# The per-head means of an encoder's projection: full-precision matmul, or two passes over split squares

## What is computed

```
xn = rms_norm(x, norm_mix)
proj = xn @ w_in                      # columns: q | k | v | ssm | two gates
q = rms_norm(q per head of 64, q_norm)    # mean over 64 channels of q*q
k = rms_norm(k per head of 64, k_norm)
q, k = rope(q), rope(k)
```

## Time and profile before

| what | value |
|---|---|
| three timed executions | 2587.70, 2590.16, 2594.99 us |
| median | 2590.16 us |
| the profiled execution, its own time | 2588.01 us |
| its span, first to last instruction | 2586.2 us |
| TensorE busy, matmuls | 2543.9 us, 98% |
| VectorE busy | 1615.3 us, 62% |
| ScalarE busy | 1044.8 us, 40% |
| POOL busy | 1306.3 us, 51% |
| mean of TensorE's granted clock | 0.995 of full speed |

### The profile page before, as it was taken

How to read it: one execution, slowest core, us unless ns; L and a number is a source line. 1 busy time by engine, 2 the same in 40 slices (tenths; PEclk the granted TensorE clock), 3 DMA queues, 4 the chain that set the end, 5 groups by cost and what they waited for, 6 DMA issues and landing times.

```text
span 2586.2 us, 38172 instructions
## 1 busy us (share of the span) xinstructions
PE 2543.9 (98%) x11174; PEld 2094.0 (81%) x11174; DVE 1615.3 (62%) x1790; ACT 1044.8 (40%) x1513; POOL 1306.3 (51%) x899
## 2 busy tenths in 40 slices
PE   7999999999899999999999999999999999999999
PEld 5777788888778888868888888788888878888887
DVE  7996288888688888866673353566453436673351
ACT  5444021221577777764442232344332334432231
POOL 3334756463567666654444444444444444454444
PEclk9999999999999999999999999999999999999999
DMA  4334132222552121124222334432222454222323
GB/s 167 110 122 143 68 90 88 86 85 76 138 146 75 46 65 49 43 92 153 98 97 95 100 119 162 158 116 97 98 98 95 137 183 146 97 94 95 99 96 122
DMA packets 132188, 274.27 MB, mean 106 GB/s; under 512 B 32896, under 2 KB 45696, under 8 KB 131968
## 3 DMA queue, kind: packets, MB, share of 16 engines
q1 hardware_dynamic: 132096, 273.12, 33.0%
HBM read 222.10 MB, written 48.76 MB: 105 GB/s over the span
## 4 chain that ended last, share of the span: by engine, by line
PE 55%; DMA 1%; POOL 0%; issue 0%; ACT 0%; DVE 0%; SPq 0%; DVEq 0%; POOLq 0%; ACTq 0%
PE t_ps L62 18%; PE t_ps L64 18%; PE t_ps L63 18%; DMA t_wraw<-w_tail_t 1%; POOL t_wlo L1942 0%; ACT t_whi L1961 0%; DVE t_x L2123 0%; PE t_ps L2157 0%; SPq L1917 0%; SPq L1882 0%; DVEq L2122 0%; SPq L1861 0%; POOLq L1941 0%; SPq L57 0%; DVEq L2046 0%
## 5 line engine op out<-in xcount | busy, mean ns | idle before, releaser
L1942 POOL TENSOR_TENSOR t_wlo<-t_wraw,t_whi 128x1024 fp32r<-128x1024 f32 x265 | 669.1, 2525 | 787.4 <-ACT t_whi L1961 787.4
L62 PE MATMUL t_ps<-block,t_whi 128*128 128x512 f32 x1920 | 748.4, 390 | 0.6 <-POOL t_wlo L1942 0.6
L64 PE MATMUL t_ps<-block,t_wlo 128*128 128x512 f32 x1920 | 746.9, 389 | 0.0
L63 PE MATMUL t_ps<-block,t_whi 128*128 128x512 f32 x1920 | 746.9, 389 | 0.0
L1961 ACT ACTIVATE t_whi<-t_wraw 128x1024 fp32r<-128x1024 f32 x265 | 280.2, 1057 | 551.4 <-PE t_ps L64 489.1
L62 PEld LDWEIGHTS t_ps<-block,t_whi 128*128 128x128 f32 x1920 | 360.4, 188 | 76.7 <-issue 2.2
L63 PEld LDWEIGHTS t_ps<-block,t_whi 128*128 128x128 f32 x1920 | 360.4, 188 | 75.8 <-issue 0.7
L64 PEld LDWEIGHTS t_ps<-block,t_wlo 128*128 128x128 f32 x1920 | 360.4, 188 | 74.7
L1552 POOL TENSOR_TENSOR a_plo<-a_p,a_phi 128x512 fp32r<-128x512 f32 x240 | 309.1, 1300 | 148.0 <-DVE a_phi L1671 140.7
L2123 DVE TENSOR_TENSOR t_x<-t_ps,t_x 128x512 f32 (+1 forms) x96 | 66.4, 692 | 373.8 <-PE t_ps L64 373.8
L2117 DVE TENSOR_TENSOR block<-t_tc,block 128x512 f32 x96 | 232.8, 2425 | 30.1 <-ACT block L2022 29.6
(11 more groups left out here) (244 smaller groups left out, 4055.4 us busy)
## 6 DMA issues: line engine op xcount, KB each, us to landing
t_wraw<-w_tail_t SPq DMA_DIRECT2D x266, 512.0 KB, 3.3
block<-roped_scratch SPq DMA_DIRECT2D x144, 128.0 KB, 2.7
w_raw<-w_in_t SPq DMA_DIRECT2D x32, 512.0 KB, 3.8
proj_scratch<-s_gate SPq DMA_DIRECT2D x48, 256.0 KB, 2.1
t_graw<-proj_scratch SPq DMA_DIRECT2D x24, 512.0 KB, 3.8
roped_scratch<-p_r_hi SPq DMA_DIRECT2D x30, 256.0 KB, 2.0
roped_scratch<-p_r_lo SPq DMA_DIRECT2D x30, 256.0 KB, 2.3
mix_scratch<-a_o SPq DMA_DIRECT2D x48, 128.0 KB, 2.4
```

The source lines that it names most:

```text
L62: pe.matmul(out, whi, xhi, start=start, stop=False)
L63: pe.matmul(out, whi, xlo, start=False, stop=False)
L64: return pe.matmul(out, wlo, xhi, start=False, stop=stop)
L1942: pool.tensor_tensor(w_lo[s][:], w_raw[s][:], f32(w_hi[s][:]), ALU.subtract).then_inc(wlo_ready, 1)
```

## The change

The squares are no longer given to a full-precision matmul. ScalarE squares a tile into `sw` and copies it, rounded to float32r, into `sq_hi`; POOL subtracts the two into `sq_lo`; TensorE makes the mean of two float32r matmuls that accumulate, one for each half. The mean matrix is loaded into `hmean_in` and copied into a float32r `hmean`. `sw` now holds first the square of one tile and later the swapped channels of another, so VectorE waits for the low half before it swaps, and ScalarE waits for a sum before it squares. POOL's order in a step is the low half and then the sine product of three steps before; its loop is cut into a first pair, four looped pairs and a rest of three sine products. To make room the buffer `o` of attention goes into the memory that is free after the gates, with a wait for the stores of the gates, and two squares of the input's norm go into other buffers.

```diff
-        self.o = [ctx.enter_context(nc.sbuf_tensor(f"a_o{s}", [HEAD, BLK], F32)) for s in range(2)]
+        self.o = [sb(f"a_o{s}", [HEAD, BLK]) for s in range(2)]
...
-        sq = sb("p1_sq", [P, 2, BLK])
-        hmean = sb("p1_hmean", [P, P])
+        hmean_in, hmean = sb("p1_hmean_in", [P, P]), sb("p1_hmean", [P, P], F32R)
+        sq_hi, sq_lo = (sb(f"p1_{n}", [P, 2, BLK], F32R) for n in ("sq_hi", "sq_lo"))
-        squares = [sq[:, 0], sq[:, 1], f32(r_lo[:, 0]), f32(r_lo[:, 1])]
+        squares = [rs[:, 2 * BLK:], qn[:, 1], f32(r_lo[:, 0]), f32(r_lo[:, 1])]
...
 ScalarE, pair():
+                    if first:
+                        act.wait_ge(rope_in, 48)
+                        act.activation(hmean[:], hmean_in[:], ACT.Copy).then_inc(hmean_set, 1)
...
-                            act.activation(sq[:, r % 2], stage[r // 3][:, cols(r % 3)],
+                            if not first or r >= 4:
+                                act.wait_ge(sum_ready, 6 * i + (r - 3))
+                            act.activation(sw[:, r % 2], stage[r // 3][:, cols(r % 3)],
                                            ACT.Square).then_inc(hsq_ready, 1)
+                            act.wait_ge(hsq_ready, 6 * i + (r + 1))
+                            act.activation(sq_hi[:, r % 2], sw[:, r % 2], ACT.Copy).then_inc(hsq_hi_ready, 1)
...
 POOL:
+                def square_low(i, r):
+                    pool.wait_ge(hsq_hi_ready, 6 * i + (r + 1))
+                    pool.tensor_tensor(sq_lo[:, r % 2], sw[:, r % 2], f32(sq_hi[:, r % 2]),
+                                       ALU.subtract).then_inc(hsq_lo_ready, 1)
+                for r in range(6):
+                    square_low(0, r)
+                    if r >= ROPE_LAG:
+                        sine(0, r - ROPE_LAG)
+                with pool.Fori(1, QK_PAIRS) as i:
                     for r in range(6):
-                        pool.wait_ge(sw_ready, 6 * i + (r + 1))
-                        pool.tensor_tensor(sw[:, r % 2], sw[:, r % 2], table[:, 1, cols(r % 3)],
-                                           ALU.mult).then_inc(sin_ready, 1)
+                        square_low(i, r)
+                        sine(i, r - ROPE_LAG)
+                for r in range(6 - ROPE_LAG, 6):
+                    sine(QK_PAIRS - 1, r)
...
 VectorE, rope():
                     dve.wait_ge(qn_ready, n + (k + 1))
+                    last = isinstance(i, int) and i == QK_PAIRS
+                    dve.wait_ge(hsq_lo_ready, NQK if last else n + (k + 3))
                     alone(dve, dve_turn)
                     dve.stream_shuffle(sw[:, s], qn[:, s], SWAP).then_inc(sw_ready, 1)
...
 TensorE, head_mean():
-                    pe.wait_ge(hsq_ready, 6 * i + (k + 1))
+                    pe.wait_ge(hsq_lo_ready, 6 * i + (k + 1))
...
-                    pe.matmul(mean[:, k % 2], hmean[:], sq[:, k % 2], start=True,
+                    pe.matmul(mean[:, k % 2], hmean[:], sq_hi[:, k % 2], start=True, stop=False)
+                    pe.matmul(mean[:, k % 2], hmean[:], sq_lo[:, k % 2], start=False,
                               stop=True).then_inc(hmean_ready, 1)
...
 attention, VectorE:
+                for c in range(NBLK):
+                    dve.wait_ge(st.gates[c], 16 * (2 * KD) + 16)
                 dve.memset(f32(v2[1][:, :, :, HEAD:P]), 0.0).then_inc(ones_set, 1)
```

More of the change, by code:

```diff
@@ L351, in project @@
         hsq_ready = sem("p1_hsq_ready")
+        hmean_set = sem("p1_hmean_set")
+        hsq_hi_ready = sem("p1_hsq_hi_ready")
+        hsq_lo_ready = sem("p1_hsq_lo_ready")
         hmean_ready = sem("p1_hmean_ready")
@@ L448, in _ @@
                     sp.dma_start(dst[:], src).then_inc(par_in, 16)
-                sp.dma_start(hmean[:], head_mean_d).then_inc(rope_in, 16)
+                sp.dma_start(hmean_in[:], head_mean_d).then_inc(rope_in, 16)
                 sp.dma_start(head_gain[:], qk_gain).then_inc(rope_in, 16)
@@ L603, in _, with sine @@
                 pool.wait_ge(rope_in, 48)
-                with pool.Fori(0, QK_PAIRS) as i:
+                def square_low(i, r):
+                    pool.wait_ge(hsq_hi_ready, 6 * i + (r + 1))
+                    pool.tensor_tensor(sq_lo[:, r % 2], sw[:, r % 2], f32(sq_hi[:, r % 2]),
+                                       ALU.subtract).then_inc(hsq_lo_ready, 1)
+                def sine(i, r):
+                    pool.wait_ge(sw_ready, 6 * i + (r + 1))
+                    pool.tensor_tensor(sw[:, r % 2], sw[:, r % 2], table[:, 1, cols(r % 3)],
+                                       ALU.mult).then_inc(sin_ready, 1)
+                for r in range(6):
[3 more added lines that the diff above has]
+                with pool.Fori(1, QK_PAIRS) as i:
                     for r in range(6):
-                        pool.wait_ge(sw_ready, 6 * i + (r + 1))
-                        pool.tensor_tensor(sw[:, r % 2], sw[:, r % 2], table[:, 1, cols(r % 3)],
-                                           ALU.mult).then_inc(sin_ready, 1)
+                        square_low(i, r)
+                        sine(i, r - ROPE_LAG)
+                for r in range(6 - ROPE_LAG, 6):
+                    sine(QK_PAIRS - 1, r)
                 n_link = [0]
@@ L862, in pair @@
                                 if first:
-                                    pe.wait_ge(rope_in, 48)
+                                    pe.wait_ge(hmean_set, 1)
                                 head_mean(i, k)
@@ L1376, in attention @@
         den = [sb(f"a_den{s}", [HEAD, BLK]) for s in range(2)]
-        o = st.o
+        o = fore.o
         ST_BANK, O_BANK, MX_BANK = 0, 2, 4
```

## The result

The changed kernel takes 2610.6 us (median of 4, 2609.5 to 2613.1) against 2589.8 us of the kernel before (median of 4). The ratio is 1.0078, with a 95% interval of 1.0066 to 1.0091: **slower by 20.8 us**. The profiled execution took 2611.1 us, its span is 2609.3 us. TensorE's matmuls are busy 2544.0 us, 97% of the span (98% before): the engine now stands idle for parts of the projection.

What follows compares the result with a forecast made beforehand. TensorE sets the pace, VectorE right behind; the change makes VectorE the bound of these pairs. Steps 20.4 us and first pair 3.1 us later, POOL's set-up ends the block 18 us late: 2608 us, range 2592 to 2622.

Steps and rivals of the forecast that it cites:

- The step times: VectorE's query and key steps: plain (no weight split) from 5.20 to 6.24 us, split from 6.37 to 7.92 us.
- the 23 steps: Second pair's first eviction to fifth pair's sixth: 16 plain and 7 split steps, 155.3 us, 20.4 more than before.
- the predicted 3.1: First pair's three roped steps: about 0.5, 1.04 and 1.55 us more, 3.1 us together.
- TensorE's gain: Two-pass means save TensorE 0.42 us a step, 12.5 us offered over 30 means; arrival depends on VectorE.
- What costs nothing: New waits of ScalarE and VectorE, the mean-matrix copy and attention's extra wait: no cost, save a few hundredths for a check.
- ScalarE's copies: 30 copies to the high half, about 0.63 us each: no cost of their own, but they stand ahead of the low half.
- The end of the block: Projection's end: POOL's state set-up, not VectorE's last weight split, ends the block, at 334.5 us.
- the 18: The projection block ends 18 us later, at 334.5 instead of 316.6 us, and nothing behind takes it back.
- The rival that the gain arrives: Low halves cost VectorE under 0.29 us a step, TensorE stays the bound, 12.5 us come off: 2578 us; chance 0.10.
- the argument against it: Against that rival: the square can't precede its eviction; the high half comes at 2.0 us, when the window is nearly over.
- the offsets: Times of a step's instructions from its eviction, taken from the kernel's own steps; gave 1.04 us more plain, 1.55 split.
- whether the shuffle blocks POOL: If VectorE's one-input shuffle blocked POOL, the low half would start 0.2 us later in plain steps, some 3 us in all.

Runs made afterwards that it cites:

- e1: Changed kernel without POOL's low half, both passes of a mean taking the high half: 2582.0 us, against 2591.4 of the kernel before.
- e2: Changed kernel with low halves still made, but the mean one full-precision matmul of the high half alone: 2612.5 us.
- e4: Changed kernel with the square in a buffer of its own, so the shuffle no longer waits for the low half: 2611.8 us.
- e11: Kernel before with only attention's buffer `o` moved and the wait for the gates' stores added, one execution: 2591.9 us.
- e5: e4 with VectorE scaling before it evicts and POOL's low half moved behind the sine product, beside the eviction: 2597.1 us.
- e3: Changed kernel with POOL subtracting one column and filling the rest of the low half by two memsets: 2586.8 us.
- e12: Kernel before with only the 12 small angle instructions of VectorE moved from behind pair 0 to before pair 4: 2587.7 us.
- e9: e5 with pair 0 in its old order, pair 1's first low half not held back, and the angle instructions before pair 4: 2587.4 us.

## Why the prediction was right

Forecast 2608.0 in 2592 to 2622, slower with 0.75; measured 2610.6. By its steps:

- **The step times.** Plain 6.24 predicted, 6.15 measured; split 7.92 and 7.84. The mechanism was the one named, the cosine product held in plain steps and L763 ahead of the low half in split ones. Both were 0.08 to 0.09 too long, 16 x 0.09 + 7 x 0.08 = 2.0 us; three plain steps took 6.30, which gives 0.5 back, so the 23 steps took 153.8 instead of 155.3. Pair 0 cost 4.25 us, 1.3 of it a later first eviction (54.15), and 2.95 of the predicted 3.1.
- **TensorE's gain.** 0.42 us a step offered (e1: 0.39), nothing arrived: e2 gives it back and loses nothing.
- **What costs nothing.** The waits (e4), the copy of the mean matrix, the wait in attention and the moved `o` (e11, one execution): confirmed. ScalarE's copies are free only in that e1 keeps them and runs 5.25 us a step; they place the low half late.
- **The end of the block.** POOL's set-up was predicted to end at 334.5 and ended at 335.83. It started 22.5 us late, as predicted (22.9), but took 76.5 us instead of 74.9: the same 172 instructions were busy 63.55 us for 61.88. I had let the chain keep its length; it shares turns with VectorE, and I take it that it met it at other places. One of its `s_pw<-s_tmp` products of 32 columns, at most 0.26 us before, took 1.27.
- **How much of the 18 is luck.** Without the later first eviction the next block is 18.1 us late, and 18 were predicted. Two errors cancel in this: POOL started 1.7 us earlier than predicted (22.5 - 1.3 = 21.2 for 22.9), and its chain took 1.7 us longer. The late first eviction and the spread of executions make up the rest to 20.8.
- **The rival that the gain arrives** asked for low halves beside the eviction. The mechanism was real (e5), but the square comes too late in this order, as the argument against it said. Its 2578 us had no term for waits at the start of the phase or for TensorE's clock; e1 got 6.7 of its 12.5 us in this block.
- **What the prediction read too narrowly.** It priced the split step by turns alone. e3 shows that 0.9 of its 1.47 us remain when the subtraction is next to nothing, and its timeline has the sine product queued behind the wait for ScalarE. The number was right because the offsets held both.
- **A reading that its rows don't show.** That an instruction with an input in PSUM takes no turns was read from the 96 equal durations of L2123. Only one of the 96 has a POOL instruction beside it, for 0.13 us, so the row says nothing on it. The statement is true all the same, by e5's evictions.

The question left open there, whether the shuffle blocks POOL, is settled: L618 started at 111.42 inside the shuffle of 110.89 to 111.63 and took 1.29 us, its free duration.

## What to carry to other kernels

Read a helper engine's instruction by what it does to the turns of the engine it is to relieve: here POOL's subtraction cost VectorE 0.95 to 1.47 us a step, more than the 0.6 us of doing it itself. Put such an instruction beside operations that read PSUM or a single SBUF operand (e5: no instruction longer for it), and be wary of putting it ahead of ready work in an in-order queue when its own input comes late (e3 suggests 0.9 us a split step). And before a saving on the engine that bounds is counted, look at the slack of the next one: it was 0.71 us a step, and the change spent more than that to save 0.42.

## What was not expected of the hardware

- A POOL subtraction of one column still waits for its turn: 0.72 us for 0.19 when VectorE's two-input product has it (e3), while memsets of 255 and 256 columns pass beside such a product at 0.31 us.
- The start of the phase is kept to its end: 12 small VectorE instructions between two pairs were worth 3.4 us of the kernel (e12: 2587.7 for 2591.1; by the interval 1.6 to 6.2), though VectorE has slack later. Its profile shows 2.0 of them in this block: first eviction 1.4 us later than before, next block 0.6 earlier.
- Ahead of the next block's first matmul TensorE stood idle for 8.18 us instead of 3.98. The matmuls then start 0.43 us apart in both kernels, up to 323.1 and 342.1 us, at a granted clock of 0.50 (1.2 GHz): the longer gap cost nothing beyond itself.
- A late mean cost TensorE twice here: behind waits of 2.6 and 2.2 us at the second pair's means its granted clock was 0.83 from 80 to 90 us (e1), behind one of 4.4 us 0.77 from 70 to 80 (e9) and behind one of 4.5 us 0.80 (the changed kernel). The kernel before, with waits of 0.4 and 1.8 us there, kept 1.00.
